# Attention projection order, state decay on ScalarE and a re-ordered expert routing in a one-core decoder-layer kernel

## The reference, cut to what matters

```
h = rmsnorm(x) * (1 + sc1) + sh1               # sc, sh, g: rows of mod = c @ w_ada + b_ada
qkv, z, b, a, cq, ckv, kpe, gates = split(h @ w_in)
qkv = silu(short_conv(qkv)); q = l2norm(q) * 128**-0.5; k = l2norm(k)
o, S = delta_rule(q, k, v, sigmoid(b), g)      # prompt: chunked; samples: S = S * exp(g) first
y_a = (rmsnorm(o) * silu(z)) @ w_o_gdn         # branch A
y_b = latent_attention(...) @ w_o_mla          # branch B
x = x + g1 * ((sigmoid(gate_a) * y_a + sigmoid(gate_b) * y_b) @ w_out)
h = rmsnorm(x) * (1 + sc2) + sh2
logits = h @ w_router + b_router               # 32 experts
top_v, top_e = top_k(logits, 4); gate = softmax(top_v)
x = x + g2 * sum over the 4 experts of gate * expert(h)
y = final_norm(x)
```

## Time and profile before

| | us |
|---|---|
| median of three runs | 1701.4 |
| profiled execution, whole | 1693.04 |
| its span in the trace | 1690.9 |
| PE busy | 1570.8 (93%) |
| PE weight loads busy | 851.8 (50%) |
| DVE busy | 503.7 (30%) |
| ACT busy | 315.2 (19%) |
| POOL busy | 23.3 (1%) |

### The profile page before, as it was taken

The page is one execution under the profiler, slowest core; times in us unless marked ns, Lnnn a source line. Parts: engine busy times, 40 slices in busy tenths (PEclk is TensorE's granted clock), DMA queues, the critical chain, the costliest instruction groups (busy, mean ns, idle before and its releaser), DMA issues. The chain is left out here.

```text
span 1690.9 us, 25648 instructions
## 1 busy us (share of the span) xinstructions
PE 1570.8 (93%) x10122; PEld 851.8 (50%) x10122; DVE 503.7 (30%) x1082; ACT 315.2 (19%) x679; POOL 23.3 (1%) x17
## 2 busy tenths in 40 slices
PE   6998688999989999699999999999999999999996
PEld 4777577576657768333433333343433333343332
DVE  1555765622310102422222222212222221222223
ACT  2222121212321100211211111111111111111112
POOL 0000300000000000000000000000000000000000
PEclk9998899999989999789999999999999999999998
DMA  9638412535349984169999999999999999999991
GB/s 403 280 137 335 188 47 110 219 113 169 100 151 339 369 350 180 53 263 429 427 426 428 427 428 428 429 428 428 429 427 428 428 426 423 428 421 427 425 416 42
DMA packets 59534, 541.25 MB, mean 320 GB/s; under 512 B 7218, under 2 KB 11442, under 8 KB 28626
## 3 DMA queue, kind: packets, MB, share of 16 engines
q1 hardware_dynamic: 58754, 534.65, 76.8%
q0 software_dynamic: 720, 5.76, 0.9%
HBM read 533.54 MB, written 6.84 MB: 320 GB/s over the span
## 5 line engine op out<-in xcount | busy, mean ns | idle before, releaser
L510 PE MATMUL banks<-ring,regA 128*64 128x512 f32 x2048 | 454.7, 597 | 0.8 <-ACT regA L568 0.8
L510 PEld LDWEIGHTS banks<-ring,regA 128*64 128x64 f32 x2048 | 144.8, 138 | 287.6 <-issue 287.6
L553 PE MATMUL banks<-ring,regC 128*64 128x512 f32 x1024 | 226.8, 595 | 0.0
L606 DVE TENSOR_TENSOR regB<-regB,banks 128x528 f32<-128x528 f32 x132 | 84.1, 700 | 383.8 <-PE banks L493 383.8
L553 PEld LDWEIGHTS banks<-ring,regC 128*64 128x64 f32 x1024 | 70.7, 137 | 131.7 <-issue 127.9
L626 DVE TENSOR_SCALAR regA<-banks 128x512 f32<-128x512 f32 x32 | 22.1, 692 | 338.5 <-PE banks L523 338.5
L571 ACT ACTIVATE regA<-regA 128x512 f32<-128x512 f32 x32 | 20.2, 632 | 516.8 <-DVE regA L626 516.8
L466 PE MATMUL banks<-regC,regA 128*64 128x512 f32 (+1 forms) x396 | 99.7, 621 | 3.3 <-DVE regA L598 3.3
L787 PE MATMUL banks<-hT,ring 128*128 128x264 f32 x384 | 90.2, 391 | 0.2 <-DMA ring<-wpre 0.2
L787 PEld LDWEIGHTS banks<-hT,ring 128*128 128x128 f32 x384 | 71.5, 190 | 18.6 <-issue 7.2
L493 PE MATMUL banks<-regA,regC 64*128 64x264 f32 x528 | 73.8, 409 | 0.7 <-ACT regC L583 0.7
(11 more groups left out here) (447 smaller groups left out, 1646.8 us busy)
## 6 DMA issues: line engine op xcount, KB each, us to landing
ring<-w_gu SPq DMA_DIRECT2D x128, 2048.0 KB, 16.2
ring<-w_dn SPq DMA_DIRECT2D x64, 2048.0 KB, 13.5
ring<-wpre SPq DMA_DIRECT2D x41, 2048.0 KB, 13.5
ring<-kvT SPq DMA_DIRECT2D x64, 256.0 KB, 4.6
ring<-kv SPq DMA_DIRECT2D x64, 256.0 KB, 6.0
ring<-ssm SPq DMA_DIRECT2D x2, 2048.0 KB, 10.8
o_ssms<-ring POOLq DMA_DIRECT2D x2, 2048.0 KB, 7.4
con_sb<-con SPq DMA_DIRECT2D x1, 1269.0 KB
```

The source lines that it names most:

```text
L510: mm = pe_mm(bank[x // 2][SLOT * (x % 2):SLOT * (x % 2 + 1), :], lhsT=hg[:, k % 4, SLOT * (k // 4):SLOT * (k // 4 + 1)], rhs=ring[c][:, 20 ...
L553: mm = pe_mm(bank[5][SLOT * y:SLOT * (y + 1), :], lhsT=actT[:, m % 4, SLOT * (m // 4):SLOT * (m // 4 + 1)], rhs=ring[c][:, D * (m % 4) + H ...
L606: V.tensor_tensor(pair, pair, banks[:, b:b + 2, 0:T], ALU.add).then_inc(acc_added, 1)
```

## The change

It has three parts.

1. *Projection and l2 norms.* `sqb` holds all 16 squares. The 16 sums (one matmul each, as before) come after the last of the 24 projections, in one row, behind one wait for all squares. The inverse roots are spread into banks 0 to 3 in place of 4, 5, 0, 1; the first waits for ACT's last copy of modulation rows, the third for DVE's last read of bank 3. The wait for all 16 products of DVE moves behind the first eight products of the delta rule, which write banks 4 and 5.
2. *Decay.* POOL's two operations are gone. ACT multiplies the 64 blocks of 128 by 128 one by one, seven ahead of a doubling level's copies: in levels 3 to 6 of c = 0 and in all levels of c = 1.
3. *Routing.* The logits are made with tokens on the partitions, so that DVE's copy and PE's turn go. PE turns the prompt's tokens right after the logits, the samples' tokens near the end. ACT copies one of six pieces, makes the exponentials and copies the rest later. The counts of tokens are PE's first products after the selection. DVE counts blocks with four operations in place of six, makes the slots (`m1T`) ahead of three copies of gates, and copies the gates' table after the first selection. PE makes 9, 6 and 2 products of 128 by 128 by 264 whose results nobody reads (`idle_products`): after the last square sum, after turning the prompt's tokens, and after the gates' table.

```diff
-L2_BANKS = (4, 5, 0, 1)
+L2_BANKS = (0, 1, 2, 3)
+DECAY_FROM = 2
+DECAY_STEP = 7
-        sqb = cut(regC, 1400, 2, T)
+        sqb = cut(regC, 3500, 2 * H, NPR)
...
-                i = m - 3
-                if 0 <= i < 2 * H:
-                    pe.wait_ge(l2sq, i + 1)
-                    pe_mm(group_sum(i, slice(0, NPR)), lhsT=row_sum(i // 4, 4), rhs=sqb[:, i % 2, 0:NPR], start=(i < 4), stop=(i >= 2 * H - 4),
-                          skip_group_check=True).then_inc(l2ss, 1)
+            pe.wait_ge(l2sq, 2 * H)
+            for i in range(2 * H):
+                mm = pe_mm(group_sum(i, slice(0, NPR)), lhsT=row_sum(i // 4, 4), rhs=sqb[:, i, :], start=(i < 4), stop=(i >= 2 * H - 4),
+                           skip_group_check=True)
+            mm.then_inc(l2ss, 1)
...
-            pe.wait_ge(l2done, 2 * H)
...
                     if g == 0 and c == 0:
                         pe.wait_ge(*once("cum_read"))
                         pe.wait_ge(stage("egB_ready"), 1)
+                        pe.wait_ge(l2done, 2 * H)
...
+            def decay(first):
+                for i in range(first, min(first + DECAY_STEP, H * NSA)):
+                    g, r = i // 32, i % 32
+                    if r == 0:
+                        act.wait_ge(stage("egB_ready"), 1)
+                        act.wait_ge(slot_in[(SSM + g) % RING], arrive[SSM + g])
+                    S = ssm_view[g][:, r // NSA, r % NSA, :]
+                    ins = A(S, S, ACT.Copy, scale=egB[:, i:i + 1])
+                    if r == 31:
+                        ins.then_inc(stage("decayed"), 1)
...
                 for lv in range(1, LEVELS):
+                    if c == 1 or lv > DECAY_FROM:
+                        decay(DECAY_STEP * ((LEVELS - 1 - DECAY_FROM if c else 0) + lv - (1 if c else DECAY_FROM + 1)))
...
-                nc.gpsimd.tensor_tensor(S, S, egB[:, 32 * g:32 * g + 32].unsqueeze(2).to_broadcast([P, 32, P]), ALU.mult).then_inc(stage("decayed"), 1)
...
-            small_projection(bank[7][0:NE, 0:T], lambda k: wsm[:, k, 16 + ROPE:WSM], 1).then_inc(once("logits_T")[0], 1)
+            def idle_products(b, n):
+                for i in range(n):
+                    pe_mm(bank[b][:, 0:T], lhsT=ones, rhs=con[:, 0:T], start=True, stop=True)
+            idle_products(3, 9)
+            for k in range(KD):
...
+                for i in range(2):
+                    pe_mm(bank[5 + i][:, 0:NE], lhsT=hT[:, k, P * i:P * i + P], rhs=wsm[:, k, 16 + ROPE:WSM],
+                          start=(k == 0), stop=(k == KD - 1), skip_group_check=True)
...
+            turn_tokens(0)
+            turn_tokens(1)
+            idle_products(4, 6)
             pe.wait_ge(stage("sel_ready"), 1)
+            pe_mm(bank[7][0:NE, 0:1], lhsT=sel[:, 0, :], rhs=ones[:, 0:1], start=True, stop=False)
...
+            turn_tokens(2)
+            pe.wait_ge(selT_copied, 1)
...
+            idle_products(6, 2)
+            pe.wait_ge(stage("h2_copied"), 6)
             moe_tensor(pe)
```

More of the change, by code:

```diff
@@ L1282, in _ @@
                     mm.then_inc(stage("h2_turned"), 1)
+            turn_tokens(0)
+            turn_tokens(1)
+            idle_products(4, 6)
             pe.wait_ge(stage("sel_ready"), 1)
+            pe_mm(bank[7][0:NE, 0:1], lhsT=sel[:, 0, :], rhs=ones[:, 0:1], start=True, stop=False)
+            pe_mm(bank[7][0:NE, 0:1], lhsT=sel[:, 1, :], rhs=ones[:, 0:1], start=False, stop=False)
+            pe_mm(bank[7][0:NE, 0:1], lhsT=sel[0:NSA, 2, :], rhs=ones[0:NSA, 0:1], start=False, stop=True).then_inc(stage("route"), 1)
+            for i, (a, b) in enumerate(tiles):
+                mm = pe.transpose(bank[4][0:NE, a:b], sel[0:b - a, i, :], ident[0:b - a, 0:b - a])
             pe_mm(bank[6][0:NE, 0:P], lhsT=sel[:, 0, :], rhs=before, start=True, stop=True)
@@ L1289, in _ @@
             pe_mm(bank[6][0:NE, NPR:T], lhsT=sel[:, 1, :], rhs=ones[:, 0:NSA], start=False, stop=False)
[L1290 to L1299, removed]
-                mm = pe_mm(bank[0][SLOT:SLOT + NE, a:b], lhsT=gate[0:b - a, i, :], rhs=ident[0:b - a, 0:b - a], start=True, stop=True,
-                           skip_group_check=True)
-            mm.then_inc(stage("route"), 1)
+            pe_mm(bank[6][0:NE, NPR:T], lhsT=sel[0:NSA, 2, :], rhs=before[0:NSA, 0:NSA], start=False, stop=True).then_inc(stage("route"), 1)
             pe.wait_ge(stage("blocks"), 1)
@@ L1305, in _ @@
             pe_mm(bank[7][0:1, 2:3], lhsT=cntc[0:NE, 0:1], rhs=ones[0:NE, 0:1], start=True, stop=True).then_inc(stage("route"), 1)
+            pe.wait_ge(stage("sel_ready"), 2)
+            pe.wait_ge(stage("h2_copied"), 4)
+            for i, (a, b) in enumerate(tiles):
+                pe.transpose(bank[3][0:NE, a:b], gate[0:b - a, i, :], ident[0:b - a, 0:b - a])
+                mm = pe_mm(bank[3][SLOT:SLOT + NE, a:b], lhsT=gate[0:b - a, i, :], rhs=ident[0:b - a, 0:b - a], start=True, stop=True,
+                           skip_group_check=True)
+            mm.then_inc(stage("route"), 1)
             pe.wait_ge(*once("e1h_ready"))
@@ L1587, in _, with copy_tokens @@
             modulate_prompt(1, hT, 24, modA2)
-            act.wait_ge(stored, 64)
-            for i in range(6):
-                act.wait_ge(stage("h2_turned"), i + 1)
-                r = slice(0, P) if i < 4 else SROW
-                A(h2tok[r, i // 2, :, 64 * (i % 2):64 * (i % 2) + 64],
-                  bank[i % 4][r, :].rearrange("p (x k) -> p k x", k=KD), ACT.Copy).then_inc(stage("h2_copied"), 1)
+            def copy_tokens(first, last):
+                for i in range(first, last):
+                    act.wait_ge(stage("h2_turned"), i + 1)
+                    r = slice(0, P) if i < 4 else SROW
+                    A(h2tok[r, i // 2, :, 64 * (i % 2):64 * (i % 2) + 64],
+                      bank[i % 4][r, :].rearrange("p (x k) -> p k x", k=KD), ACT.Copy).then_inc(stage("h2_copied"), 1)
+            act.wait_ge(stored, 64)
+            copy_tokens(0, 1)
             act.wait_ge(*once("v8_ready"))
@@ new lines, in _, with copy_gates @@
+            dve.wait_ge(*once("items_ready"))
+            def copy_gates():
+                dve.wait_ge(stage("route"), 7)
+                for i, r in tok_tiles:
+                    ins = V.tensor_copy(gg[r, i, :], bank[4][r, NJ1 * i:NJ1 * (i + 1)])
+                    if i < 2:
+                        link(ins)
+                    else:
+                        ins.then_inc(stage("rg_copied"), 1)
+                dve.wait_ge(stage("rg_copied"), 1)
+            moe_vector(dve, copy_gates)
```

85 lines of the change are left out of this document (39 added, 46 removed).

## The result

The changed kernel took 1663.85 us, the median of four runs (1661.72 to 1666.10), beside 1702.69 for the kernel before: a ratio of 0.977 (95% interval 0.975 to 0.979), 38.8 us less. The forecast was 1662.0. The profiled executions differ by less: 1693.04 before, 1664.52 after, 28.5 us. So the total was right, and the sum of 39.4 us that led to it was not. The table follows PE through both traces; a landmark's shift includes all that went before it.

What follows compares the result with a forecast made beforehand. The expert loop, with PE busy and DMA at 1.00, was the greater part, so only its earlier start counted. 9.3 + 2.0 + 12.1 + 16.0 = 39.4 us off the median 1701.4 gave 1662.0 us, range 1652 to 1675.

Steps and rivals of the forecast that it cites:

- I take the gain from the median: Last step: 39.4 us, worked out on the profiled execution of 1693.04, subtracted from the runs' median 1701.4, giving 1662.0.
- Sums, 9.3: Projections: 16 sums moved behind the loop fall from 10.9 to 2.2 us and hide a 0.61 us wait; gain 9.3.
- five chunks would be there in time: Behind the projections: the chunk loaded last has the sums and five modulation chunks to arrive under; no size given.
- sums don't overlap: Rival at the sums behind the projections: they cost 0.68 us each as before, 9.3 us less gain, 1671.3; chance 0.05.
- Products ahead of the wait, 2.0: Start of the delta rule: the first sixteen products run during PE's 1.98 us wait for DVE; gain 2.0 us.
- Decay, 12.1: Delta rule: without POOL's operations c = 0 falls from 35.73 to 23.63 us, ACT's decays being hidden; gain 12.1.
- The rival's price: Rival in the delta rule: ACT's decays show at 0.52 us each, 8.7 us less gain, 1670.7; chance 0.05.
- Routing, 16.0: Last square sum through first expert chunk: shorter chain and full clock, 3.3 + 1.6 + 2.5 + 1.7 + 1.7 + 5.2 us.
- The clock's rival: Routing: the clock falls all the same between the second and third unused products; 6.5 us left, 1671.5; chance 0.17.
- DVE right behind its clearing: Sign in the routing: DVE's first logit step comes right behind its own last clearing; the term's gain is 3.3 us.
- 1.00 throughout: Sign in the routing: PE's clock stays at 1.00 from the last square sum to the first expert.
- any wait that eats the earlier start: Sign of being wrong: any new wait ahead of the expert loop that uses up the earlier start; no size given.

## Why the prediction was right, and where it was not

- **Total.** 1662.0 against 1663.85, by two errors that cancel; that they did is luck. The terms promised 39.4 us and the profiles' spans show 28.2: 5.0 us are missing in the sums, 0.5 in the products ahead of the wait, 2.3 behind c = 0, 1.4 in the routing and 1.1 in the expert loop, and after starts its projections 0.9 us later. The step "I take the gain from the median" supposed that before's median and its profiled execution, 8.4 us apart, lie the same way in after. They don't: after's profiled execution lies 0.7 us above its median. Before's later runs have a lower mean clock (0.959 to 0.975) than after's (0.977 to 0.983), and what a run loses by that was nowhere in the working. Which stage cost before's longer runs their time wasn't seen in a profile of before. The four runs of before beside the result, 1700 to 1704, were among the longer ones; in the next comparison of the two kernels the difference was 35.3. And the runs of before spread by 1.5%, where the prediction took 0.2% as what can be told from none.
- **Sums, 9.3.** The passes cost 1.91 us (2.2 predicted) and the modulation starts 10.5 us earlier, counted from the projections' start. The term failed behind that: it said that five chunks would be there in time, which they were, and didn't ask what PE's waits "for issue" in the modulation were. They grew from 2.8 to 6.9 us, and PE came to the spreads at low clock: from the projections' start 4.3 of the 10.5 us were left there. What is new is above all the first wait, 2.33 us. In before PE passes that place without a stop, and DMA had stood at 0.00 from 130 to 136 us, up to the start of the modulation; in after the loads start at 125 us, under the sums. From one wait's end to the next one's, 126 passes on, it is 6.2 us in before and 6.4 and 7.0 in after. That the earlier loads are why the first wait appeared fits these rows and the run with the loads held back, but no run shows it by itself. The rival "sums don't overlap" was wrong: it had 10.9 us for the passes that took 1.91.
- **Products ahead of the wait, 2.0.** Right: in the kernel with this part alone the shift grows from 5.3 us at the spreads to 7.35 behind them, in after from 3.46 to 4.98.
- **Decay, 12.1.** Right to 0.1 us, in after and alone. Hidden by 0.64 us (0.5 predicted). On the rule of the Trainium skill ("ScalarE: Activation LUTs", Rules for kernel authors) the trace has its number: ACT's idle time took the blocks at 0.31 us each, and DVE, the late engine, got nothing more. No run puts the decay on DVE, so what the rule would cost here isn't shown. The rival's price was too high: it took every excess over 2.67 us a level as lost, and fourteen decays cost 0.3 us a level on average, not 1.5. Of the 12.1 us 1.4 were lost between the chunks and 0.8 in c = 1, where PE worked at low clock in after (0.50 from 210 to 212 us, 0.55 from 240 to 242).
- **Routing, 16.0.** 14.6: 11.9 up to the first expert and 2.7 in its first chunk. Step by step: up to DVE's first logit step 1.9 (3.3 predicted), to the counts 3.6 (1.6 + 2.5), to the gather 2.8 (1.7 + 1.7), gather to first expert 3.6 and chunk 2.7 (2.4 + 2.8). These are gains on one execution of before: on its second profile, 4.9 us shorter here, they would be 9.7, and the three further profiles of the old routing are near the first. The clock's rival was half right: it did fall, but among the logits, between the first and the second group of unused products, and it came back during the second. The Trainium skill's statement on turns in transpose mode ("TensorE: Matmul & The Clock Gate", Part 4) is not decided: in the kernel before the clock stays at 1.00 through the sixteen turns (from 693.74 us) and until 702, which doesn't show it falling by them, and in after and its variants the turns run at low clock or behind unused products.
- **What would show it.** Confirmed: sums in a row (1.91 us, a little under the 2 to 2.5), c = 0, seven decays, first chunk. Failed: DVE right behind its clearing, 1.00 throughout, and "any wait that eats the earlier start", which is what the modulation's waits were.

## What to carry to other kernels

A sum of terms made on one profiled execution should be set beside several executions' times and mean granted clocks: where a kernel's runs spread by 1%, a stage that the change doesn't touch can give back or add more than the change. Look for the waits of a microsecond or two ahead of long uninterrupted matmul work, and fill them if PE has nothing else; too many fillers make PE itself late. Ask of every wait of PE that no semaphore ends, in a stretch of many short passes, how busy DMA is there: moving work ahead of the stretch can bring it under the loads, and holding loads back can take such waits away.

## What the runs showed of the hardware that I had not expected

- PE's clock can stay at 0.50 through 33 us of uninterrupted work of one kind (products of 32 rows by 512 columns and of 128 by 264), in three of these profiles; the same work ran at 1.00 in nine others, after the same wait of 1.85 to 1.87 us.
- It fell at 674 us with PE's records, whose ends are modelled, filled for 2.99 of the 3 us from 670 on, two thirds of it by products of 32 columns, for which ACT makes five of the eight tiles at 0.51 us each; three unused products of 264 columns among them kept it at 1.00.
- In the modulation of after PE stood still for 1.7 to 2.9 us every 126 short passes while DMA was at 1.00, and at the last two of these places not at all with DMA at 0.13.
